# The same products with the weights' columns streamed from the last to the first, in a 256-token encoder layer

## The chip, the cores and the metric

One core of one Trainium2 chip runs the whole program. Time is device time in microseconds, from the start of the execution to its end; the kernel before took 2340.43 us (median of 3 runs, 2340.24 to 2341.03).

## The reference

One encoder layer for 256 tokens of width 2048, in float32:

```python
x = x + 0.5 * swiglu_ffn(rms_norm(x, g1), w_gate, w_up, w_down)        # 2048 -> 5632 -> 2048
h = rms_norm(x, g_mix)
u = h @ w_in       # conv (2 x 2048), q_down 768, kv_down 512, k_rope 64, two gates of 2048
y_conv = conv_branch(u_conv)      # glu, 31-tap depthwise conv, layer norm, silu, @ w_pw_out
y_mla = mla_branch(c_q, c_kv, k_rope)  # 16 heads, latent attention, @ w_o
x = x + (sigmoid(gl_conv) * y_conv + sigmoid(gl_mla) * y_mla) @ w_out
x = x + 0.5 * swiglu_ffn(rms_norm(x, g2), w_gate2, w_up2, w_down2)
return rms_norm(x, g_final)
```

Nearly all of the arithmetic is products of the 256 tokens with weight matrices that are used once.

## The kernel before

Weights are stored by the host in *units*: a unit holds two blocks (`DEEP` = 2) of 128 rows of a weight matrix by 512 columns (`WIDE`), so that each of the 128 partitions gets 1024 float32. There are 814 units. A *group* is one block of 512 output columns over the full depth of a matrix: 8 units for depth 2048, 22 for depth 5632. One group, the last of `latents`, is 320 columns wide. `units_of` (L1256) makes the units, `column_groups` (L1262) goes over the blocks of columns of one or two matrices. The 32 units of `heads` are made by another function, `head_units`.

Each unit goes through four steps, one engine each, in a ring of four slots (`SLOTS`):

- SyncE loads it into `raw` once VectorE is done with what was in the slot.
- ScalarE writes it as float32r (a float32 rounded to fewer bits) into `w_hi` (`round_unit`, L431), once TensorE has used the unit that was in the slot before (`unit_used`).
- VectorE writes the rest, `raw` minus `w_hi`, into `w_lo` (`split_unit`, L926).
- TensorE waits for `lo_ready` and multiplies.

The activations are split in the same way in a high and a low part. `multiply` (L678) makes a product of three matmuls: high by high (L681), high by low (L682), low by high (L683), accumulated in one bank. The *stationary* operand, loaded first, is 128 rows by 128 tokens of the activations (`h`, `hidden`, `attn`, `merged`, `c_q`); the *moving* operand, streamed through the array, is the 512 columns of the weights. `wide_unit` (L770) does one unit: for each of the two blocks `r` and each of the two halves of the tokens `tt` one `multiply`, so 12 matmuls. 782 of the units go through it. The heads go through `head_pair`, which takes its weights by `block_of` as the stationary operand, or as the moving one in blocks of 256 columns; the attention itself multiplies plain float32.

The order of the work on every engine is written out by hand by unit number: after certain units TensorE transposes finished results (`turn_group`, L692), and ScalarE and VectorE evict banks, make norms and the convolution's taps. The output columns of a group lie in two banks, `banks(g)`, one for each half of the tokens, and all that follows reads them in rising order. SyncE's queue holds the loads in the order of the units.

Of the kernel before, what the change touches and what calls it, by code (L numbers as in the profile page):

```python
# [14 lines left out]
P = 128  # L15
# [20 lines left out]
DEEP = 2  # L36
# [127 lines left out]
def encoder(nc, streams, xt_in, x_in, pos_in, gains_in, final_in, taps_in, const_in, freq_in, out):  # L164
# [6 lines left out]
    with ExitStack() as ctx:  # L171
        def sb(name, shape, dt=F32, stack=ctx):
            return stack.enter_context(nc.sbuf_tensor(name, shape, dt))
# [5 lines left out]
        w_hi = sb("w_hi", [P, SLOTS, UNIT], F32R)  # L179
        w_lo = sb("w_lo", [P, SLOTS, UNIT], F32R)  # L180
# [156 lines left out]
        def banks(g):  # L337
            return bank[2 * g.pair], bank[2 * g.pair + 1]
# [337 lines left out]
        def _(pe):  # L676

            def multiply(dst, fixed, moving, first, last):  # L678
                fixed_hi, fixed_lo = fixed
                moving_hi, moving_lo = moving  # L680
                pe.matmul(dst, fixed_hi, moving_hi, start=first, stop=False)  # L681
                pe.matmul(dst, fixed_hi, moving_lo, start=False, stop=False)  # L682
                return pe.matmul(dst, fixed_lo, moving_hi, start=False, stop=last)  # L683
# [66 lines left out]
            def wait_stationary(g, k):  # L750

                if g.stage == "ffn1_up":
                    pe.wait_ge(xt_lo, k + 2)
                elif g.stage in ("ffn1_down", "ffn2_down"):
                    pe.wait_ge(turn_lo, low_turned(g.stage[:4] + "_up", ("up",), k))
                elif g.stage == "conv_in":
                    pe.wait_ge(turn_lo, low_turned("ffn1_down", ("resid",), k))
                elif g.stage == "q_rope":
                    t = turns[plan.q_turn]
                    pe.wait_ge(turn_lo, t.lo_before + t.lo)  # L760
                elif g.stage == "mla_out":
                    pe.wait_ge(head_lo, k + 2)
                elif g.stage == "conv_out":
                    pe.wait_ge(ln_lo, k // 2 + 1)
                elif g.stage == "w_out":
                    pe.wait_ge(turn_lo, low_turned("conv_out", ("merge",), k))
                elif g.stage == "ffn2_up":
                    pe.wait_ge(turn_lo, low_turned("w_out", ("resid",), k))

            def wide_unit(u, g):  # L770
                fixed = STATIONARY[g.stage]
                slot, w = u % SLOTS, g.width
                pe.wait_ge(lo_ready, u + 1)
                if g is plan.stage(g.stage)[0]:
                    wait_stationary(g, DEEP * (u - g.u0))
                for r in range(DEEP):
                    k = DEEP * (u - g.u0) + r
                    moving = w_hi[:, slot, r * w:(r + 1) * w], w_lo[:, slot, r * w:(r + 1) * w]
                    for tt in range(2):
                        tokens = slice(tt * P, (tt + 1) * P)  # L780
                        last = multiply(banks(g)[tt][:, 0:w], (fixed[:, k, 0, tokens], fixed[:, k, 1, tokens]), moving,
                                        k == 0, k == g.deep - 1)
                last.then_inc(unit_used, 1)
# [103 lines left out]
            while u < n_units:  # L887
                if H0 <= u < M0:
                    head_pair((u - H0) // 4)
                    u += 4  # L890
                    continue
                if u == M0:
                    attend_scores(PAIRS - 1)
                if u in plan.starts:
                    wait_banks(plan.starts[u])
                    g = groups[plan.starts[u]]
                wide_unit(u, g)
                turn_after(u)
                if u == Q_END + LATE_TURN_AFTER:
                    late_turns()  # L900
                if u == M0:
                    attend_values(PAIRS - 2)
                if u == M0 + 3:
                    attend_turn(PAIRS - 1)
                if u == M0 + 4:
                    attend_values(PAIRS - 1)
                if FORE <= u < FORE + 8:
                    fore(u - FORE)
                if BACK <= u < BACK + 8:
                    back(u - BACK)  # L910
                u += 1
# [344 lines left out]
def units_of(w):  # L1256

    k, width = w.shape
    return w.reshape(k // (DEEP * P), DEEP, P, width).transpose(0, 2, 1, 3).reshape(-1, P, DEEP * width)

def column_groups(*weights):  # L1262

    cuts = range(0, weights[0].shape[1], WIDE)
    return np.concatenate([units_of(w[:, c:c + WIDE]) for c in cuts for w in weights], 0)
# [85 lines left out]
```

## Time and profile before

| | |
|---|---|
| median of the timed runs | 2340.43 us |
| profiled execution | 2340.69 us |
| its span, first to last instruction | 2338.9 us |
| TensorE matmuls busy | 2312.5 us, 10718 records |
| TensorE weight loads busy | 1923.4 us |
| VectorE busy | 1322.0 us |
| ScalarE busy | 1188.5 us |
| read from HBM | 428.78 MB |

A matmul's listed duration holds the time in which its last columns drain, and the next one starts before that is over; the distance from start to start says how fast TensorE goes on.

### The profile page before, as it was taken

How to read it: one execution, taken by the hardware profiler on the slowest of the kernel's cores; microseconds unless marked ns; L12 is line 12 of the kernel's file. 1: busy time of each engine (PE TensorE's matmuls, PEld its weight loads, DVE VectorE, ACT ScalarE, POOL GpSimd, SP SyncE). 2: the span in 40 equal slices, each digit the busy share in tenths (PEclk: the TensorE clock that was granted, in tenths of full speed). 3: DMA queues.
4: the chain of work that ended last, by engine and by line, in shares of the span. 5: the costliest groups of instructions: out<-in, count | busy, mean ns of one | idle time of the engine just before them, and what ended most of it. 6: DMA issues, size and time to landing. Idle time of an engine off the chain costs nothing.

```text
span 2338.9 us, 26788 instructions
## 1 busy us (share of the span) xinstructions
PE 2312.5 (99%) x10718; PEld 1923.4 (82%) x10718; DVE 1322.0 (57%) x1470; ACT 1188.5 (51%) x1620; POOL 0.2 (0%) x4
## 2 busy tenths in 40 slices
PE   8999999999999999999999999999999999999997
PEld 7888888888888888878889888888888888888886
DVE  5545544544545488997875465555544544544443
ACT  6444444444444577787776564444444444443343
POOL 0000000000000000000000000000000000000000
PEclk9999999999999999999999999999999999999999
DMA  8666666665656666566643456666666666666664
GB/s 287 188 189 192 187 189 191 188 188 188 183 187 183 194 190 183 178 193 186 196 139 116 144 172 188 185 185 207 189 187 191 189 187 192 188 188 189 188 188 128
DMA packets 121532, 432.65 MB, mean 185 GB/s; under 512 B 13632, under 2 KB 13888, under 8 KB 121280
## 3 DMA queue, kind: packets, MB, share of 16 engines
q1 hardware_dynamic: 121408, 430.93, 60.3%
q8 instruction: 85, 1.39, 0.3%
q14 instruction: 39, 0.32, 0.0%
HBM read 428.78 MB, written 2.10 MB: 184 GB/s over the span
## 4 chain that ended last, share of the span: by engine, by line
PE 97%; DVE 1%; ACT 1%; issue 1%; DMA 0%; SPq 0%; ACTq 0%; DVEq 0%
PE bank L681 31%; PE bank L683 31%; PE bank L682 31%; PE turned L692 2%; PE bank L824 1%; PE bank L798 1%; PE bank L799 1%; DVE q_rope L1116 0%; PE turned L809 0%; ACT w_hi L431 0%; DVE w_lo L926 0%; DVE q_rope L1122 0%; DMA raw<-in_ffn_up 0%; PE turned L878 0%; ACT q_rope L539 0%
## 5 line engine op out<-in xcount | busy, mean ns | idle before, releaser
L926 DVE TENSOR_TENSOR w_lo<-raw,w_hi 128x1024 fp32r<-128x1024 f32 (+2 forms) x814 | 986.6, 1215 | 967.8 <-ACT w_hi L431 967.5
L431 ACT ACTIVATE w_hi<-raw 128x1024 fp32r<-128x1024 f32 (+2 forms) x814 | 853.3, 1052 | 1011.4 <-PE bank L683 1004.8
L681 PE MATMUL bank<-w_hi,h 128*128 128x512 f32 (+1 forms) x2144 | 836.0, 390 | 10.3 <-DVE w_lo L926 10.3
L683 PE MATMUL bank<-w_hi,h 128*128 128x512 f32 (+1 forms) x2144 | 832.9, 388 | 0.0
L682 PE MATMUL bank<-w_lo,h 128*128 128x512 f32 (+1 forms) x2144 | 832.8, 388 | 0.0
L681 PEld LDWEIGHTS bank<-w_hi,h 128*128 128x128 f32 x2144 | 403.2, 188 | 93.3 <-DVE w_lo L926 11.6
L683 PEld LDWEIGHTS bank<-w_hi,h 128*128 128x128 f32 x2144 | 403.0, 188 | 82.9
L682 PEld LDWEIGHTS bank<-w_lo,h 128*128 128x128 f32 x2144 | 403.3, 188 | 81.4
L681 PE MATMUL bank<-w_hi,hidden 128*128 128x512 f32 x704 | 278.9, 396 | 0.0
L682 PE MATMUL bank<-w_lo,hidden 128*128 128x512 f32 x704 | 278.4, 395 | 0.0
L683 PE MATMUL bank<-w_hi,hidden 128*128 128x512 f32 x704 | 278.4, 395 | 0.0
L683 PEld LDWEIGHTS bank<-w_hi,hidden 128*128 128x128 f32 x704 | 132.4, 188 | 32.0
L682 PEld LDWEIGHTS bank<-w_lo,hidden 128*128 128x128 f32 x704 | 132.4, 188 | 31.7
L681 PEld LDWEIGHTS bank<-w_hi,hidden 128*128 128x128 f32 x704 | 132.4, 188 | 31.6
L539 ACT ACTIVATE q_rope<-padded,taps 128x256 f32<-128x256 f32 x320 | 135.8, 498 | 1.0 <-DVE q_rope L1116 1.0
L1116 DVE TENSOR_TENSOR q_rope<-q_rope 128x1024 f32<-128x1024 f32 x76 | 92.5, 1217 | 0.0
L1122 DVE SCALAR_TENSOR_TENSOR q_rope<-padded,taps,q_rope 128x256 f32<-128x256 f32 x160 | 66.6, 477 | 0.0
L681 PE MATMUL bank<-w_hi,attn 128*128 128x512 f32 x128 | 52.4, 410 | 0.0
L458 ACT ACTIVATE opened<-bank,rstd 128x512 f32<-128x512 f32 x52 | 33.0, 685 | 37.4 <-PE bank L683 37.4
L681 PE MATMUL bank<-w_hi,merged 128*128 128x512 f32 x128 | 50.6, 395 | 0.0
L683 PE MATMUL bank<-w_hi,merged 128*128 128x512 f32 x128 | 50.2, 392 | 0.0
L683 PE MATMUL bank<-w_hi,attn 128*128 128x512 f32 x128 | 50.2, 392 | 0.0
(171 smaller groups left out, 1219.3 us busy)
## 6 DMA issues: line engine op xcount, KB each, us to landing
raw<-in_ffn_up SPq DMA_DIRECT2D x352, 512.0 KB, 4.0
raw<-in_ffn_down SPq DMA_DIRECT2D x176, 512.0 KB, 3.7
raw<-in_conv_in SPq DMA_DIRECT2D x64, 512.0 KB, 3.8
raw<-in_conv_gate SPq DMA_DIRECT2D x32, 512.0 KB, 4.1
raw<-in_mla_gate SPq DMA_DIRECT2D x32, 512.0 KB, 4.1
raw<-in_mla_out SPq DMA_DIRECT2D x32, 512.0 KB, 3.6
raw<-in_conv_out SPq DMA_DIRECT2D x32, 512.0 KB, 3.6
raw<-in_w_out SPq DMA_DIRECT2D x32, 512.0 KB, 3.6
```

What stands on the lines that cost most here:

```text
L431: act.activation(w_hi[:, j, 0:n], raw[:, j, 0:n], ACT.Copy).then_inc(hi_ready, 1)
L458: act.activation(opened[:, tt, :], banks(g)[tt][:, :], func, scale=rstd[:, tt:tt + 1]).then_inc(by_act, 1)
L539: act.activation(conv_prod[made % 2][:, r, :], padded[:, m, t:t + T], ACT.Copy, scale=taps[:, m, t:t + 1]).then_inc(tap_made, 1)
L681: pe.matmul(dst, fixed_hi, moving_hi, start=first, stop=False)
L682: pe.matmul(dst, fixed_hi, moving_lo, start=False, stop=False)
L683: return pe.matmul(dst, fixed_lo, moving_hi, start=False, stop=last)
L692: last = pe.transpose(turned_bank[n % 2][:, r * T + tt * P:r * T + (tt + 1) * P], src[:, tt, c:c + P], identity[:, :])
L798: pe.matmul(dst, q_nope[:, j, cols], k_nope[:, j, :], start=True, stop=False)
L799: last = pe.matmul(dst, q_rope[:, p, 0, cols], k_rope[:, j, :], start=False, stop=True)
L926: dve.tensor_tensor(w_lo[:, j, 0:n], raw[:, j, 0:n], w_hi[:, j, 0:n], ALU.subtract).then_inc(lo_ready, 1)
L1116: dve.tensor_tensor(dst, conv_acc, conv_prod[made % 2], ALU.add).then_inc(tap_done, 1)
L1122: dve.scalar_tensor_tensor(out=conv_acc[:, r, :], in0=padded[:, m, t:t + T], scalar=taps[:, m, t:t + 1], in1=conv_acc[:, r, :], op0=ALU.mu ...
```

## The change

The host stores the columns of each group of 512 (or 320) in reverse order, and `wide_unit` streams them with a step of minus one, so that they enter TensorE in the same order as before and each result lands in the same column of the bank. The first block's slice runs from 511 down to 0, the second's from 1023 down to 512. The heads' units and matmuls stay as they are.

```diff
--- before.py
+++ after.py
@@ -775,7 +775,9 @@
                     wait_stationary(g, DEEP * (u - g.u0))
                 for r in range(DEEP):
                     k = DEEP * (u - g.u0) + r
-                    moving = w_hi[:, slot, r * w:(r + 1) * w], w_lo[:, slot, r * w:(r + 1) * w]
+
+                    backwards = slice((r + 1) * w - 1, r * w - 1 if r else None, -1)
+                    moving = w_hi[:, slot, backwards], w_lo[:, slot, backwards]
                     for tt in range(2):
                         tokens = slice(tt * P, (tt + 1) * P)
                         last = multiply(banks(g)[tt][:, 0:w], (fixed[:, k, 0, tokens], fixed[:, k, 1, tokens]), moving,
@@ -1256,7 +1258,7 @@
 def units_of(w):
 
     k, width = w.shape
-    return w.reshape(k // (DEEP * P), DEEP, P, width).transpose(0, 2, 1, 3).reshape(-1, P, DEEP * width)
+    return w[:, ::-1].reshape(k // (DEEP * P), DEEP, P, width).transpose(0, 2, 1, 3).reshape(-1, P, DEEP * width)
```

## Rows read from the trace of the kernel before

**Rows 1.** Page: busy us (share) xcount; chain by engine and line; a DMA issue.

```profile
PE 2312.5 (99%) x10718; PEld 1923.4 (82%) x10718; DVE 1322.0 (57%) x1470; ACT 1188.5 (51%) x1620; POOL 0.2 (0%) x4
...
PE 97%; DVE 1%; ACT 1%; issue 1%; DMA 0%; SPq 0%; ACTq 0%; DVEq 0%
PE bank L681 31%; PE bank L683 31%; PE bank L682 31%; PE turned L692 2%; PE bank L824 1%; PE bank L798 1%; PE bank L799 1%; DVE q_rope L1116 0%; PE turned L809 0%; ACT w_hi L431 0%; DVE w_lo L926 0%; DVE q_rope L1122 0%; DMA raw<-in_ffn_up 0%; PE turned L878 0%; ACT q_rope L539 0%
...
raw<-in_ffn_up SPq DMA_DIRECT2D x352, 512.0 KB, 4.0
```

**Rows 2.** Waits: who waited for whom: us in total, times, longest.

```profile
ACT w_hi L431 <- PE bank L683: 1004.8, 635, 2.2
DVE w_lo L926 <- ACT w_hi L431: 967.5, 668, 3.2
...
PE bank L681 <- DVE w_lo L926: 10.3, 4, 8.4
```

**Rows 3.** Timeline of TensorE from 69.65 us: start, duration; first and last of 37.

```profile
69.65 0.39 PE L683 MATMUL bank<-w_hi,h 128*128 128x512 f32 x1
...
77.81 0.39 PE L683 MATMUL bank<-w_hi,h 128*128 128x512 f32 x1
```

**Rows 4.** Timeline of TensorE from 559.79 us: first and last of 31.

```profile
559.79 0.39 PE L683 MATMUL bank<-w_hi,hidden 128*128 128x512 f32 x1
...
566.79 0.40 PE L683 MATMUL bank<-w_hi,hidden 128*128 128x512 f32 x1
```

**Rows 5.** Timeline of TensorE: first and last of 23 (320 columns), of 17 (256).

```profile
972.71 0.31 PE L683 MATMUL bank<-w_hi,h 128*128 128x320 f32 x1
...
975.93 0.31 PE L681 MATMUL bank<-w_hi,h 128*128 128x320 f32 x1
...
1203.78 0.28 PE L682 MATMUL bank<-w_lo,c_kv 128*128 128x256 f32 x1
...
1205.66 0.28 PE L683 MATMUL bank<-w_hi,c_kv 128*128 128x256 f32 x1
```

**Rows 6.** Cores: span and mean granted clock of TensorE.

```profile
core 0: 2338.9 us, clock 0.998
```

**Rows 7.** Timeline of TensorE from 8.94 us: first and last of 12.

```profile
8.94 0.63 PE L682 MATMUL bank<-w_lo,h 128*128 128x512 f32 x1
...
13.64 0.61 PE L681 MATMUL bank<-w_hi,h 128*128 128x512 f32 x1
```

**Rows 8.** Groups by shape: xcount, busy us, mean ns, idle before.

```profile
L926 DVE TENSOR_TENSOR w_lo<-raw,w_hi 128x1024 fp32r<-128x1024 f32 x790 | 965.1, 1224 | 940.1 <-ACT w_hi L431 939.8
L431 ACT ACTIVATE w_hi<-raw 128x1024 fp32r<-128x1024 f32 x790 | 834.0, 1059 | 1001.7 <-PE bank L683 995.2 <-DMA raw<-in_ffn_up 2.2 <-DMA raw<-in_mla_out 1.1
L681 PE MATMUL bank<-w_hi,h 128*128 128x512 f32 x2112 | 826.1, 391 | 10.3 <-DVE w_lo L926 10.3
...
L681 PEld LDWEIGHTS bank<-w_hi,h 128*128 128x128 f32 x2144 | 403.2, 188 | 93.3 <-DVE w_lo L926 11.6
...
L681 PE MATMUL bank<-w_hi,hidden 128*128 128x512 f32 x704 | 278.9, 396 | 0.0
...
L681 PE MATMUL bank<-w_hi,attn 128*128 128x512 f32 x128 | 52.4, 410 | 0.0
L681 PE MATMUL bank<-w_hi,merged 128*128 128x512 f32 x128 | 50.6, 395 | 0.0
...
L681 PE MATMUL bank<-w_hi,h 128*128 128x320 f32 x32 | 9.9, 309 | 0.0
L681 PE MATMUL bank<-w_hi,c_q 128*128 128x512 f32 x24 | 9.5, 396 | 0.0
```

**Rows 9.** Timeline of TensorE: float32 matmuls; first and last of six pairs.

```profile
1208.40 0.59 PE L799 MATMUL bank<-k_rope,q_rope 128*128 128x256 f32 x2
...
1210.56 0.59 PE L798 MATMUL bank<-k_nope,q_nope 128*128 128x256 f32 x2
```

## The prediction

> **What bounds the kernel now.** I read the page's busy times first, then the chain of waits, then the waits themselves, and last the starts of single matmuls in the timeline. TensorE is busy 2312.5 us of a span of 2338.9 us, and the chain that ended last is 97% TensorE, 93% of it the three lines of `multiply` [rows 1]. VectorE (57%) and ScalarE (51%) have room. The longest waits are ScalarE waiting for a slot to be freed by TensorE (1004.8 us) and VectorE waiting for ScalarE's rounded copy (967.5 us); TensorE itself waited for `w_lo` 10.3 us in all, 8.4 us of it once, at the start [rows 2]. So neither the transfers nor the two preparing engines set the end; whatever changes the pace of TensorE's matmuls changes the time one for one, and whatever changes only the others is hidden.
>
> What matters then is not the listed duration of a matmul (390 ns, with its drain) but the distance from start to start. In the stage of `h` 36 steps take 77.81 - 69.65 = 8.16 us, 226.7 ns each [rows 3]. With `hidden` as the stationary operand 30 steps take 7.00 us, 233.3 ns each, though the shape is the same [rows 4]. With 320 columns 22 steps take 3.22 us, 146.4 ns; with 256 columns (the heads) 16 steps take 1.88 us, 117.5 ns [rows 5]. The mean granted clock is 0.998 of full, which is the 2.4 GHz level [rows 6]; 512 columns at one a cycle are 213.3 ns, so 13.3 ns are not streaming (20.0 ns with `hidden`, 13.0 ns with 320 columns, 10.8 ns with 256). The very first matmuls ran at the lower level, 1.2 GHz: 11 steps in 4.70 us, 427.3 ns each [rows 7], which is 512/1.2 = 426.7 ns and no rest to speak of. So the kernel streams one column per cycle of TensorE's clock at either level.
>
> **The change part by part.** On the host the columns of each group are stored in reverse. That work is outside the device time. The arrays keep their shape, each load still moves 512 KB in 4.0 us [rows 1], and ScalarE's rounding (1059 ns a unit) and VectorE's subtraction (1224 ns a unit) read and write as before, forward, the same number of elements [rows 8]. A unit feeds 12 matmuls, 12 x 226.7 = 2720 ns, so even these two durations in a row (2283 ns) fit under one unit of TensorE, and in fact they overlap it with four slots. Cost 0; if they were not hidden they would cost nothing either, since nothing about them changes. The loads' waits and their order in SP's queue are untouched, and no wait is added or moved on any engine.
>
> On TensorE the moving operand of `wide_unit` gets a step of -1 instead of +1, starting at the last element of the 512. The count of instructions stays: 782 wide units of 12 matmuls are 9384, which the lines confirm: L681 has 2112 + 704 + 128 + 128 + 24 matmuls of 512 columns and 32 of 320, 3128, and L682 and L683 as many, 3 x 3128 = 9384 [rows 8]. The loads of the stationary operand (188 ns each) keep their direction and stay beside the matmul before. The output is written forward to the same bank as before. The heads' matmuls, through `block_of` and `head_units`, are not touched, nor the transposes and the plain-float32 attention.
>
> So the sum is 9384 times one number: what a descending read adds to a step of 226.7 ns. No row of this trace has a descending operand. Its bounds:
> - Above, with two prices. A stream that gave one element per 1.2 GHz cycle would have the pace of rows 7, 427.3 ns: 200.6 ns more for each of 6336 steps on `h`, 194.0 for each of 2112 on `hidden`, about 199 for the other 840 of 512 columns, and 120 for each of the 96 of 320 (320/1.2 = 266.7 less 146.4). That is 1271 + 410 + 167 + 12 = 1860 us. And the kernel has matmuls that go slower yet: the attention's operands, plain float32, show two records for each matmul of the code, and 5 pairs of them take 1210.56 - 1208.40 = 2.16 us, 432 ns for 256 columns, four cycles a column [rows 9]. If a descending operand lost the fast float32r path altogether, 512 columns would take 864 ns, and the sum were 9384 x 0.636 = 5970 us.
> - Below: the steps can't go under their 213.3 ns of streaming, 13.3 x 9384 = 125 us less. A smaller and nearer figure: if `hidden` came to the pace of `h`, 2112 x 6.7 ns = 14 us less. Nothing in the change aims at this, but I have no reason for the 6.7 ns, so I can't exclude it.
>
> I take 0. The rate of the stream is the clock's (one column per cycle at both levels), every element lies directly beside the one before it in either direction, and the reading side makes no difference between operands that start at different places in the slot (`r` = 0 or 1, both among the steps of rows 3). The nearest row by what is done (same type, same count, same bytes) is rows 3 itself, with 226.7 ns; rows 7 is another clock and rows 9 another type.
>
> The skill bears on this. "Advanced Engine Details and Errata", section "SBUF Cachelines", in the Trainium skill says that the on-chip memory is read in lines of 16 bytes, that accesses falling into the same line run at full speed and that two hits on a line suffice to cover its latency. By that, four float32 in a line give four hits in either direction, and the sum is 0 too. The page names no direction, and no row here separates a rule about hits from one about lines fetched ahead, upward only; so I give it some weight and not all.
>
> The time of the profiled execution was 2340.69 us, its span 2338.9 and 1.8 us around it; the median of the three timed runs is 2340.43. The forecast is 2338.9 + 1.8 + 0 = 2340.7 for that execution, and 2340.4 against the median.
>
> **The rivals.**
> A. *The reader of the moving operand fetches pairs or lines upward only.* Then a descending stream gives one element per slow cycle, and the pace is that of rows 7: 2340 + 1860 = 4200 us. For it: float32r streams 2.4 G elements of 4 bytes a second, twice what the plain-float32 records do per record (256 columns in 216 ns, [rows 9]), so something in the fast path moves two elements at a time, and such a thing may want them in rising order. Against: nothing in the trace shows the mechanism. Its stronger form, the loss of the whole float32r path, gives 8300 us.
> B. *Each descending operand pays at its start.* The first element lies at the far end of the operand's last line, and the stream crosses the reads of the stationary operand, which run upward, instead of running along with them. For it: the 13.3 ns that are not streaming exist, and they change by 6.7 ns with the stationary tile alone [rows 3, 4], so the pace does depend on where the two operands are read. 6.7 ns on all is 9384 x 0.0067 = 63 us, 2403 us; the whole rest once more, 13.3 ns, is 125 us, 2465 us. Against: the rest is almost gone at the lower clock [rows 7] and is nearly the same for 512 and 320 columns, which looks like a fixed handover between matmuls and not like reads in each other's way. It decides from 0.5 ns a matmul on, since 9384 x 0.0005 = 4.7 us is 0.2% of the time.
> C. *The same coupling goes the other way*: `hidden` comes down to the pace of `h`, 14 us, 2326 us. For it stands only that the difference exists; against, that only the moving side changes, which is one and the same for both tiles.
> D. *The change doesn't do what it says*: the step is turned round on its way into the instruction, or read as rising with the columns swapped elsewhere. It would cost nothing, and the time would be the forecast's. It is within the forecast.
>
> **How the numbers follow.** Forecast, with D: 50%. B: 22%, mostly near its lower price. A: 20%, of which 2 are the stronger form. C: 8%. The range takes in the forecast and B in full (to 2468 us) and C down to 2324 us; out of it lies A, 20%. The forecast's own range is 2337 to 2344. What a measurement of this kernel can tell from no change is 0.2%, 4.7 us. So: faster 8%, within 50%, slower 42%. Cases of one sign and none hold most of the chance; the likeliest alone would be a range of a few microseconds.
>
> **What would show it.** In the profile after, 36 steps at 70 us should again take 8.16 us, 30 steps at 560 us 7.00 us, and the heads' 256-column steps 117.5 ns whatever happens elsewhere. If A holds, the `multiply` groups show long matmuls at a full granted clock, the steps are 427 ns and the heads keep 117.5; by its stronger form the count of TensorE instructions rises from 10718 as well. If B holds, all wide steps grow by the same few nanoseconds, for 320 columns as for 512, and TensorE's waits in rows 2 stay small. If instead VectorE's or ScalarE's unit became longer, or TensorE began to wait for `w_lo`, the claim that only TensorE sees the change is wrong. The forecast falls if the wide steps differ from theirs before by more than 0.5 ns.

## The result, and the profile after

The changed kernel took 2384.91 us (median of 4 runs, 2384.57 to 2385.57) against 2340.63 us for the kernel before: a ratio of 1.019, 95% interval 1.0175 to 1.0204. It is slower by 44.3 us, 1.9%. The profiled span went from 2338.9 to 2382.8 us.

The page of the changed kernel (busy us, share, records; the chain by engine; one group of loads of the stationary tile), its cores view and two of its waits, which answer to [rows 1], [rows 6] and [rows 2]:

```profile
PE 2356.9 (99%) x10718; PEld 1925.2 (81%) x10718; DVE 1322.9 (56%) x1470; ACT 1187.2 (50%) x1620; POOL 0.2 (0%) x4
...
PE 97%; DVE 1%; ACT 1%; issue 1%; DMA 0%; SPq 0%; ACTq 0%; DVEq 0%
...
L681 PEld LDWEIGHTS bank<-w_hi,h 128*128 128x128 f32 x2144 | 403.8, 188 | 105.5 <-DVE w_lo L928 10.9
```

```profile
core 0: 2382.8 us, clock 0.998
```

```profile
ACT w_hi L431 <- PE bank L683: 1044.4, 638, 2.2
DVE w_lo L928 <- ACT w_hi L431: 1006.7, 673, 3.2
...
PE bank L681 <- DVE w_lo L928: 9.8, 4, 8.1
```

The count of records is the same, VectorE and ScalarE are busy as long as before and only wait longer for TensorE, TensorE waits for them as little as before, and the granted clock is the same. A load of a stationary tile is listed with 188 ns as in [rows 8]. So the time went into TensorE's own pace. The timeline of the changed kernel shows where: first and last of 37 matmuls on `h`, of 31 on `hidden`, of 36 with 320 columns, and of 11 at the very start.

```profile
69.40 0.40 PE L683 MATMUL bank<-w_hi,h 128*128 128x512 f32 x1
...
77.80 0.40 PE L683 MATMUL bank<-w_hi,h 128*128 128x512 f32 x1
...
559.80 0.40 PE L683 MATMUL bank<-w_hi,hidden 128*128 128x512 f32 x1
...
566.80 0.40 PE L683 MATMUL bank<-w_hi,hidden 128*128 128x512 f32 x1
...
992.76 0.31 PE L681 MATMUL bank<-w_hi,h 128*128 128x320 f32 x1
...
997.90 0.31 PE L683 MATMUL bank<-w_hi,h 128*128 128x320 f32 x1
```

```profile
8.73 0.63 PE L682 MATMUL bank<-w_lo,h 128*128 128x512 f32 x1
...
13.00 0.61 PE L683 MATMUL bank<-w_hi,h 128*128 128x512 f32 x1
```

And 37 matmuls on `merged`, first and last, in the kernel before and then in the changed one:

```profile
1577.69 0.39 PE L683 MATMUL bank<-w_hi,merged 128*128 128x512 f32 x1
...
1585.93 0.39 PE L683 MATMUL bank<-w_hi,merged 128*128 128x512 f32 x1
```

```profile
1533.52 0.40 PE L683 MATMUL bank<-w_hi,merged 128*128 128x512 f32 x1
...
1541.92 0.40 PE L683 MATMUL bank<-w_hi,merged 128*128 128x512 f32 x1
```

On `h` 36 steps take 8.40 us, 233.3 ns each, against 226.7 in [rows 3]. On `hidden` 30 steps take 7.00 us as in [rows 4]: nothing changed where the step was already 233.3. With 320 columns 35 steps take 5.14 us, 146.9 ns, against 146.4 in [rows 5]; from starts read to the nanosecond the two are within 0.1 ns of each other, so nothing changed there either. At the lower clock, 1.2 GHz, 10 steps take 4.27 us, 427 ns, as in [rows 7] (the trace's record of the clock begins only at 14.1 us, 13.5 us in the changed kernel; the level ahead of it is read from the pace). On `merged` 36 steps took 8.24 us, 228.9 ns, and now take 8.40 us, 233.3 ns; `attn` went the same way. From the starts of the stages: the first up stage is 13.5 us longer (490.6 to 504.1), the second 13.8, `conv_in` 4.9, the two gates 4.6, all other stages together 7.2, the two down stages 0.0: 44.1 us. The stages on `h` together are 40.6 us of it. The price of 6.67 ns on all 6336 steps would be 42 us; a unit that comes right after transposes paid less of it (its mean step went from 236.9 to 241.1 ns).

### The profile page after: what moved, and what is told of

Read it like the earlier page. It is cut to its first block, busy times and chain, and to the rows that moved or that the text cites. A ratio compares the mean times of both kernels' runs of the same rounds, so it can differ in the third digit from the quotient of the medians.

```text
span 2382.8 us, 26788 instructions
## 1 busy us (share of the span) xinstructions
PE 2356.9 (99%) x10718; PEld 1925.2 (81%) x10718; DVE 1322.9 (56%) x1470; ACT 1187.2 (50%) x1620; POOL 0.2 (0%) x4
## 4 chain that ended last, share of the span: by engine, by line
PE 97%; DVE 1%; ACT 1%; issue 1%; DMA 0%; SPq 0%; ACTq 0%; DVEq 0%
PE bank L681 31%; PE bank L683 31%; PE bank L682 31%; PE turned L692 2%; PE bank L826 1%; PE bank L800 1%; PE bank L801 1%; DVE q_rope L1118 0%; PE turned L811 0%; ACT w_hi L431 0%; DVE w_lo L928 0%; DVE q_rope L1124 0%; DMA raw<-in_ffn_up 0%; PE turned L880 0%; ACT q_rope L539 0%
## 5 line engine op out<-in xcount | busy, mean ns | idle before, releaser
L681 PE MATMUL bank<-w_hi,h 128*128 128x512 f32 (+1 forms) x2144 | 853.2, 398 | 9.8 <-DVE w_lo L928 9.8
L682 PE MATMUL bank<-w_lo,h 128*128 128x512 f32 (+1 forms) x2144 | 850.3, 397 | 0.0
L683 PE MATMUL bank<-w_hi,h 128*128 128x512 f32 (+1 forms) x2144 | 850.1, 396 | 0.0
L681 PE MATMUL bank<-w_hi,merged 128*128 128x512 f32 x128 | 51.0, 398 | 0.0
L682 PE MATMUL bank<-w_lo,attn 128*128 128x512 f32 x128 | 50.8, 397 | 0.0
```

## The experiments

In the two maps each group of the two up stages (8 units of 12 matmuls) reads its operands in another way, all in one kernel; the rest of the kernel is as before. The number given for a way is the time from the first to the last start within a unit, over 11, as the median of the group's eight units, from starts that the trace holds to the nanosecond. The products of these groups come out with other columns or tokens, or cut short. "Stream +s" is the moving operand begun s elements later (both blocks `r` then read the unit's first block), "tile +s" the stationary tile; an element is 4 bytes.

**m1_map.** The kernel before with this in place of the two slices:

```diff
-                    moving = w_hi[:, slot, r * w:(r + 1) * w], w_lo[:, slot, r * w:(r + 1) * w]
+                    cols = tile[:, slot, r * w + shift:r * w + shift + w]       # tile: w_hi, w_lo
+                    # descending:      cols[:, ::-1]
+                    # blocks of b:     cols.rearrange("p (a b) -> p a b", b=b)[:, ::-1, :]
+                    # falling inside:  cols.rearrange("p (a b) -> p a b", b=b)[:, :, ::-1]
+                    # step 2:          cols.rearrange("p (a b) -> p b a", b=2)
```

> The kernel before, with the operands of the 22 groups of the first and of the second up stage read in 22 different ways each (8 units of 12 matmuls to a way); the products of these groups come out in another order of columns or of tokens, so only the distances between starts are read. Theory 1 (position): a step is 512 columns (213.3 ns) and a handover of 13.3 or 20.0 ns, and which it is depends on where the first element that is streamed and the first element of the stationary tile lie within 256 bytes; the direction matters only because a descending stream starts at the other end of the block. Then ascending streams with the stationary tile moved by 16, 32 or 48 elements give 233.3 or 229.2 ns in places, as hidden, attn and merged do, and some descending streams with a moved tile give 226.7. Theory 2 (direction): a descending stream costs 6.7 ns by itself unless it is paid already; then all descending ways give 233.3 whatever the shift, all ascending ones on h 226.7, one descending operand of three (low part only) gives about 228.9, two of three 231.1, and half of the blocks 230.0. Blocks of 16 or 64 in descending order that rise inside tell whether the inner step or the start decides.

| way (stationary tile `h`) | ns a step |
|---|---|
| ascending | 226.6 |
| descending | 233.4 |
| descending, high part only / low part only | 233.5 / 229.0 |
| descending, first block only / first half of tokens only | 232.1 / 234.7 |
| ascending, stream +1, +4, +8, +16, +32, +48 | 236.6, 232.0, 233.2, 228.6, 232.9, 233.4 |
| blocks of 256 / 64 from last to first, rising inside | 226.6 / 226.7 |
| blocks of 16 / 4 from last to first, rising inside | 233.4 / 233.3 |
| blocks of 256 / 16 rising, falling inside | 233.4 / 266.6 |
| ascending, tile +4, +8, +12, +16, +24 | 226.7, 233.5, 233.4, 233.5, 234.3 |
| ascending, tile +32, +40, +48, +56 | 232.9, 233.6, 228.9, 233.2 |
| ascending, stream and tile both +16, +32, +48 | 226.7, 226.6, 226.6 |
| ascending, stream +16, tile +48 | 232.9 |
| descending, tile +8, +16, +24, +32, +40, +48, +56 | 233.4, 233.2, 233.1, 240.0, 233.3, 233.3, 233.3 |
| descending, stream +1, +4, +16 | 235.5, 233.4, 233.4 |
| even columns, then odd (step 2) | 451 |

Its timeline, first and last of 12 matmuls of one unit each: tile +16; stream and tile both +16; tile +48; blocks of 64; step 2.

```profile
1725.69 0.40 PE L681 MATMUL bank<-w_hi,h 128*128 128x512 f32 x1
...
1728.26 0.39 PE L683 MATMUL bank<-w_hi,h 128*128 128x512 f32 x1
...
2044.89 0.39 PE L681 MATMUL bank<-w_hi,h 128*128 128x512 f32 x1
...
2047.38 0.39 PE L683 MATMUL bank<-w_hi,h 128*128 128x512 f32 x1
...
1816.63 0.39 PE L681 MATMUL bank<-w_hi,h 128*128 128x512 f32 x1
...
1819.15 0.39 PE L683 MATMUL bank<-w_hi,h 128*128 128x512 f32 x1
...
336.55 0.39 PE L681 MATMUL bank<-w_hi,h 128*128 128x512 f32 x1
...
339.04 0.39 PE L683 MATMUL bank<-w_hi,h 128*128 128x512 f32 x1
...
301.26 0.63 PE L681 MATMUL bank<-w_hi,h 128*128 128x512 f32 x1
...
306.22 0.63 PE L683 MATMUL bank<-w_hi,h 128*128 128x512 f32 x1
```

The distances are 2.57, 2.49, 2.52, 2.49 and 4.96 us. Moving the tile by 64 bytes costs the descending price with an ascending stream, and moving the stream by the same 64 bytes takes the price away again. Tile +48 is the same relation as stream +16 (192 bytes, or 64 the other way), and both give 229, the value of `attn`, `merged` and `c_q`, which lie just so; tile +16 is `hidden`'s relation and gives `hidden`'s value. So the three values of before are explained by the distance between tile and stream within 256 bytes. Theory 2 falls as it was stated: ascending streams pay too, and a stream that goes through its operand from the far end in blocks of 256 bytes does not. Of its prices for mixed ways one came (229.0 ns with the low part alone descending); the others did not (233.5 where it said 231.1; 232.1 and 234.7 where it said 230.0). Theory 1 holds for the place and fails for the direction: no descending stream came down to 226.7, so a descending stream is not merely one that starts at another place.

**m2_map.** The same with finer shifts and other widths.

```diff
-                    cols = tile[:, slot, r * w + shift:r * w + shift + w]
+                    cols = tile[:, slot, r * w + shift:r * w + shift + min(w, wide)]   # wide: 496 to 384
```

> A second map: the kernel before with 22 more ways in each of the two up stages; the products of these groups come out shifted, reversed or cut short, so only the distances between starts are read. Ascending with the stream's start moved by 2 to 64 elements, the tile moved by 1 to 60; descending with the tile moved by 1 to 62; and both directions at 496, 480, 448 and 384 columns. Theory 1 (position, in 256 bytes): a shift of the stream by 64 elements gives 226.7 again, since only the place within 256 bytes counts; shifts of one end and of the other answer each other (stream +s like tile -s). Descending is 233.3 or more at every shift, or there is a place not tried yet that gives 226.7; then the direction never cost anything and the place is all. Widths: a step is the streaming plus a handover of 13.3 ns ascending at every width; descending 20.0 ns at 496 to 384 columns if the cost belongs to the handover, and down to 13.3 somewhere on the way if it grows with the length of the stream, since 320 columns showed no difference between the two directions.

Ascending, stream +64 gave 226.7, +63 and +60 226.6; +2, +3, +5, +12, +20, +24, +28, +40, +44, +52 and +56 gave 228.8 to 235.9. Ascending, tile +1, +2, +3, +5, +6 and +60 gave 232.4, 230.6, 226.6, 233.4, 230.8 and 226.7; both +1 gave 237.5. At steps of 8 elements, moving the stream one way answers moving the tile the other way, within 1 ns, as theory 1 said. At finer steps it does not: stream +4 and tile +60 are the same distance and gave 232.0 and 226.7, and both +1 is no distance at all. Descending, tile +1 to +6, +12, +20, +28, +36, +44, +52, +60 and +62 gave 233.2 to 236.7. With those of the first map that makes 22 places of the tile, and none of them gives a descending stream the faster pace.

| columns | streaming at 2.4 GHz | ascending | descending | difference |
|---|---|---|---|---|
| 496 | 206.7 | 223.5 | 226.5 | 3.0 |
| 480 | 200.0 | 216.7 | 220.0 | 3.3 |
| 448 | 186.7 | 202.6 | 207.0 | 4.4 |
| 384 | 160.0 | 173.4 | 177.9 | 4.5 |

First and last of 12 matmuls with 384 columns, ascending, then descending, in this kernel's timeline:

```profile
463.26 0.33 PE L681 MATMUL bank<-w_hi,h 128*128 128x384 f32 x1
...
465.17 0.33 PE L683 MATMUL bank<-w_hi,h 128*128 128x384 f32 x1
...
480.11 0.34 PE L681 MATMUL bank<-w_hi,h 128*128 128x384 f32 x1
...
482.07 0.34 PE L683 MATMUL bank<-w_hi,h 128*128 128x384 f32 x1
```

With 6.7 ns at 512 columns and 0 at 320, the cost of descending is not a fixed price at the start of each matmul. Nor does the difference simply shrink with the width, since both directions have a say in it. What a descending step holds beyond its streaming is about 20 ns from 512 down to 448 columns, 17.9 at 384 and 13.3 at 320; the expectation had allowed for that. The ascending rest, which it put at 13.3 ns at every width, is that at 512, 384 and 320 columns, and 15.9 to 16.8 at 448 to 496.

**x4_h_moved.** Nothing descends; only `h` lies elsewhere.

```diff
+        sb("before_h", [P, 16])
         h = sb("h", [P, KT, 2, T], F32R)
...
-        sb("before_hidden", [P, 8])
+        sb("before_hidden", [P, 8 + 48])
```

> The kernel before (ascending), with h alone moved by 64 bytes (and 192 bytes of unused room behind it, so that every other large tile keeps its place within 256 bytes). Theory 1: the steps on h go from 226.7 to 233.3 ns though nothing descends, 6336 x 6.7 = 42 us more, 2383 us, all but the same as the reversed kernel's 2384.9. Theory 2: 2340.6 us.

Measured 2381.40 us, ratio 1.0174 (1.0161 to 1.0188). Its timeline, first and last of 37 on `h`:

```profile
69.34 0.39 PE L684 MATMUL bank<-w_hi,h 128*128 128x512 f32 x1
...
77.74 0.39 PE L684 MATMUL bank<-w_hi,h 128*128 128x512 f32 x1
```

8.40 us for 36 steps, 233.3 ns. By placing one tile 64 bytes further, 40.9 of the 44.3 us appear without any reversal.

**x5_blocks64.** The columns fall in blocks of 256 bytes.

```diff
-                    moving = w_hi[:, slot, backwards], w_lo[:, slot, backwards]
+                    moving = tuple(t[:, slot, r * w:(r + 1) * w].rearrange("p (a b) -> p a b", b=BLOCK)[:, ::-1, :]
+                                   for t in (w_hi, w_lo))                                   # BLOCK = 64
...
-    return w[:, ::-1].reshape(k // (DEEP * P), ...
+    w = w.reshape(k, width // BLOCK, BLOCK)[:, ::-1, :]
+    return w.reshape(k // (DEEP * P), ...
```

> The changed kernel, with the columns stored and streamed in blocks of 64 (256 bytes), the blocks from the last to the first and each block rising inside. Theory 1: every block begins at the same place within 256 bytes as an ascending stream would, so the pace of before comes back, 2340.6 us. A theory in which the way through the operand as a whole (its start at the far end, the blocks falling) costs the time: 2384.9 us.

Measured 2340.45 us, ratio 0.9999 (0.9991 to 1.0008). Its timeline, first and last of 37 on `h`:

```profile
69.34 0.39 PE L684 MATMUL bank<-w_hi,h 128*128 128x512 f32 x1
...
77.50 0.39 PE L684 MATMUL bank<-w_hi,h 128*128 128x512 f32 x1
```

8.16 us as in [rows 3]. Neither the far start nor the falling order of the parts costs anything here; the falling inside 256 bytes does.

**x1_aligned.** Every stationary tile at the weights' place within 256 bytes.

```diff
-        sb("before_hidden", [P, 8])
+        sb("before_hidden", [P, 56])
...
         conv = padded[:, :, PAD:PAD + T]
+        sb("before_attn", [P, 32])
```

> The kernel before (ascending), with 192 bytes of unused room more ahead of hidden and 128 ahead of attn and merged (which moves c_kv and c_q too), so that each stationary tile starts at the same place within 256 bytes as the weights' slots (128). Theory 1 (position of stationary against moving): hidden goes from 233.3 to 226.7 ns a step, attn, merged and c_q from 229.2 to 226.7; 2112 x 6.7 + 840 x 2.5 ns = 16.2 us less, 2324.4 us. Theory 2 (only the direction counts, and hidden is slow for another reason, for instance its depth of 44 or its length): 2340.6 us as before.

Measured 2326.81 us, ratio 0.9941 (0.9929 to 0.9954). Its timeline, first and last of 31 on `hidden`, then of 33 in the heads:

```profile
570.05 0.39 PE L684 MATMUL bank<-w_hi,hidden 128*128 128x512 f32 x1
...
576.85 0.39 PE L684 MATMUL bank<-w_hi,hidden 128*128 128x512 f32 x1
...
1193.22 0.28 PE L682 MATMUL bank<-c_kv,w_hi 128*128 128x256 f32 x1
...
1197.06 0.28 PE L684 MATMUL bank<-w_hi,c_kv 128*128 128x256 f32 x1
```

`hidden` now takes 6.80 us for 30 steps, 226.7 ns, and the two down stages are 6.9 and 7.0 us shorter. The gain is 13.7 us and not the expected 16.2. Of the missing 2.5 us some 1.5 went to the heads: their matmuls of 256 columns, whose tiles had moved along, went to 3.84 us for 32 steps, 120.0 ns, against about 118 before, and the stretch from the start of `q_rope` to `mla_out`, which holds the heads, grew from 144.2 to 145.6 us. Much of the rest is `mla_out`, which gained 0.3 us only, where 384 steps at 2.5 ns had been put at 1.0.

**x6_aligned_back.** The changed kernel with the two lines of x1_aligned.

> The changed kernel (descending) with the tiles placed as in x1_aligned. Theory 1 with what the map showed (a descending stream was at 233 ns or more at all nine places of the tile that were tried): no gain from the placing, 2384.9 us. If descending cost a fixed 6.7 ns on top of what the place costs, hidden would now gain too and the time would be near 2384.9 - 2112 x 0 - ... the same for h and 226.7 + 6.7 for hidden, so also 2384.9; what tells is hidden's step, which may not rise to 240. A time under 2375 us would say that the place still matters for descending streams.

Measured 2385.96 us, ratio 1.0194 (1.018 to 1.0208). First and last of 31 on `hidden`:

```profile
559.72 0.40 PE L683 MATMUL bank<-w_lo,hidden 128*128 128x512 f32 x1
...
566.72 0.40 PE L683 MATMUL bank<-w_lo,hidden 128*128 128x512 f32 x1
```

233.3 ns, not 240 and not 226.7. So for `hidden` the descending price is not added to the place's price, and a good place doesn't take it away. The maps have two places where a descending stream does cost more: 240.0 ns with tile +32, 236.7 with tile +36. The time is 1.1 us above the changed kernel's; the stretch with the heads is 1.6 us longer, as it had grown in x1_aligned.

**x8_c64, x9_c192, x10_c0.** x1_aligned with the heads' tiles `c_kv` and `c_q` at each of the other three places.

```diff
+        sb("before_c_kv", [P, 48])        # 16 in x9_c192, 32 in x10_c0
         c_kv = sb("c_kv", [P, KVT, 2, T], F32R)
```

> x1_aligned (2326.8 us), with c_kv and c_q alone put back to the place within 256 bytes that they had before (64, against 128 of the weights), by 192 bytes of unused room. In x1_aligned the heads' steps of 256 columns went from 117.5 to 120.0 ns. If a place can be good for 512 columns and bad for 256, the heads return to 117.5: 672 x 2.5 = 1.7 us less, 2325.1 us. If the heads' loss came from something else, 2326.8.

> As x8_c64, with c_kv and c_q at 192 (64 above the weights, where 512 columns take 233.3 ns). By a rule of lockstep alone the heads' 256 columns would be slowest here, 120 ns or more; the rule is not known for this width, so the step is what is asked.

> As x8_c64, with c_kv and c_q at 0 (128 away from the weights). The heads' step of 256 columns is between 113 and 120 ns; the fourth of the four places.

x8_c64 took 2325.13 us, ratio 0.9936 (0.9923 to 0.995), the fastest of all. The other two were run once each: 2326.23 and 2326.34 us. The stretch with the heads took 144.2 us with the tiles at 64, 144.6 at 192, 145.7 at 0 and 145.6 at 128. That stretch also holds 72 steps of 512 columns on `c_q`, which follow their own order; without them it is 127.7 us at 64, 127.8 at 192, 129.0 at 0 and 129.3 at 128. So for 256 columns the place that is best for 512 is the worst, and 192, where 512 columns take 233.5 ns, is as good as 64. The steps with `c_kv` as the stationary tile, taken alone, are 117.4 ns as a mean at 64, 114.5 at 192, 118.4 at 0 and 120.0 at 128. The guess of the expectation for x9_c192 was wrong. First and last of 33 in the heads of x8_c64, then of 13 with `c_kv` stationary in x9_c192:

```profile
1192.48 0.28 PE L683 MATMUL bank<-c_kv,w_hi 128*128 128x256 f32 x1
...
1196.25 0.28 PE L685 MATMUL bank<-w_hi,c_kv 128*128 128x256 f32 x1
```

```profile
1197.06 0.28 PE L683 MATMUL bank<-w_hi,c_kv 128*128 128x256 f32 x1
...
1198.42 0.28 PE L683 MATMUL bank<-w_hi,c_kv 128*128 128x256 f32 x1
```

3.77 us, 117.8 ns, and 1.36 us, 113.3 ns.

## Why the prediction was wrong

What bounds the kernel was right: only TensorE's pace changed, ScalarE and VectorE were busy as long as before, and the change in time is the change in the steps.

The step that failed is "I take 0": the one term of the sum was put at nothing, and it measured 6.7 ns on `h`, 4.4 on `attn`, `merged` and `c_q`, and nothing on `hidden` or with 320 columns. Of its three grounds the first two hold but don't decide: the stream is one column a cycle in either direction, and neighbours lie side by side. The third, that "the reading side makes no difference between operands that start at different places in the slot (`r` = 0 or 1)", was no test: the two starts are 2048 bytes apart, the same place within 256 bytes, and the maps show that it is this place, taken against the tile's, that counts. The rows that did test it stood beside it, 226.7 against 233.3 ns for the same shape [rows 3, 4], and they were used only for a rival and a lower bound. The measured time does lie between the ends of the prediction's range, 2324 and 2468 us, but only because the range took in rival B; the forecast itself said no change.

Rival B had the right kind of mechanism, a coupling of the two reads, and its nearer price, 6.7 ns, was right for `h`. That a bad place and a falling stream cost the same 6.7 ns was not reasoned, so there was luck in it. Its sum was off: it laid the price on all 9384 matmuls, 63 us, where the 2112 on `hidden` were already paying it and the 320-column ones never do; 6336 x 6.7 + 840 x 4.4 ns (`attn`, `merged` and `c_q`) = 46.1 us was the sum, against 44.3 measured. Its picture of a payment at each start, at the far end of the operand, was wrong, as x5_blocks64 and the steps of 320 columns show. Its objection, that a rest which is nearly the same for 512 and 320 columns looks like a fixed handover, misled me: ascending at one place of the tile the rest is 13.3 to 16.8 ns over the widths, and at 512 columns it is 13.3 to 21.0 by the tile's place alone.

Rival A (half pace) did not come: descending pairs stream at one column a cycle. But what was said for it is real, since a step of two elements does halve the pace (451 ns). Rival C ran the wrong way for this change, yet its 14 us exist: x1_aligned takes them by placing the tile, with no reversal. Rival D, a reversal that never reaches the instruction's reads, is out, since the pace changed.

The Trainium skill's rule ("Advanced Engine Details and Errata", "SBUF Cachelines"), that two hits on a 16-byte line are enough to cover the memory's latency, spoke for 0. It does not hold for this operand: with a step of two float32r elements each line still gets two hits, and the step measured 451 ns against 226.7. So four hits on a line were no ground for a cost of 0 either.

What stays open: why the pace depends on where both operands are read. A load is listed with 188 ns in both kernels, so the profile does not say which of the two reads is held up. Shown is that the pace depends on the tile's place against the stream's within 256 bytes, that the direction costs nothing on `h` at the 1.2 GHz level (427 ns either way; other tiles were not seen at that level), that a stream falling all the way was at the good pace at none of 22 places of the tile with 512 columns, and that the good place differs by width. That two reads of opposite or shifted course meet in the same part of the memory would fit, but nothing here shows such parts. A tile read in reverse as well was not tried.

## What to carry to other kernels

When TensorE is the bound, compare the distance from start to start of matmuls of one shape across their stationary tiles: if it differs, the tiles' places are a cost, and some bytes of unused room ahead of a tile win time without any other change (here 192, 128 and 192 bytes for 15 us of 2340, 0.64%). Try the places rather than work them out: the best one differs between 512 and 256 columns. Keep the moving operand rising and dense inside 256 bytes; its larger blocks may come in any order, as far as 64 and 256 elements show. A row that varies without a reason is evidence against "this costs nothing", and an average price belongs only on the instructions that don't pay it yet.

## What the runs showed of the hardware that was not expected

- With 512 float32r columns and a tile loaded for each, a step is 226.7 ns when tile and stream start at the same place within 256 bytes (and with the tile moved by 3, 4 or 60 elements), 229 with the tile 192 bytes further on, 231 to 236 at most others; with the stream begun one element off, 236.6 ns.
- With 256 columns and `c_kv` as the tile the order is another: 120.0 ns at the same place, 114.5 with the tile 64 bytes further on.
- Descending costs 6.7 ns at 512 columns against the best place, 3.0 to 4.5 at 384 to 496, nothing at 320. Rising blocks of 64 or 256 elements taken from last to first cost nothing.
- A stream with a step of two elements takes 451 ns, twice the dense one; rising blocks of 16 that fall inside take 266.6 ns.
